# HGRN2 near scores as 32x32 diagonal blocks, levels 6 and 7 as single blocks, and one 256-column ones product in stick-breaking attention

## The reference

```
b = cumsum(log f)
scores[t,s] = sum_d q[t,d] * k[s,d] * exp(b[t,d] - b[s,d])      (s <= t)
o = scores @ v   (the reference does it chunk by chunk with a carried state)
```

```
within = cumsum(log_keep, axis=keys, reverse=True) - log_keep
later  = cumsum(block totals, reverse=True) - block totals
w = exp(log_sigmoid(z) + within + later)
```

## Time and profile before

| | |
|---|---|
| median of 3 runs | 1402.86 us (1402.77 to 1404.02) |
| the profiled execution's own time | 1402.92 us |
| its span in the profile | 1401.4 us |
| PE busy (MATMUL) | 1394.3 us, 99% of the span, 9682 records |
| PEld busy (LDWEIGHTS) | 1285.5 us, 92% |
| DVE busy | 1030.6 us, 74% |
| ACT busy | 754.0 us, 54% |
| POOL busy | 143.4 us, 10% |

### The profile page before, as it was taken

The page is one execution under the profiler, slowest core; times in us unless marked ns, Lnnn a source line. Parts: engine busy times, 40 slices in busy tenths (PEclk is TensorE's granted clock), DMA queues, the critical chain, the costliest instruction groups (busy, mean ns, idle before and its releaser), DMA issues.

```text
span 1401.4 us, 27481 instructions
## 1 busy us (share of the span) xinstructions
PE 1394.3 (99%) x9682; PEld 1285.5 (92%) x9682; DVE 1030.6 (74%) x1409; ACT 754.0 (54%) x1050; POOL 143.4 (10%) x190
## 2 busy tenths in 40 slices
PE   9999999999999999999999999999999999999999
PEld 8999999999999999988888888888888888888888
DVE  7898866699898777776687777777777776445453
ACT  7584777654543454545555555555555554344332
POOL 1200000000000014322111111111111110000000
PEclk9999999999999999999999999999999999999999
DMA  8654545454555556665556656656656656666663
GB/s 280 191 181 168 162 153 184 147 168 165 189 178 174 195 171 223 223 192 194 170 197 196 189 186 192 192 180 193 191 187 193 190 177 194 208 185 202 194 206 109
DMA packets 75935, 261.66 MB, mean 187 GB/s; under 512 B 8736, under 2 KB 9280, under 8 KB 75872
## 3 DMA queue, kind: packets, MB, share of 16 engines
q1 hardware_dynamic: 74304, 256.41, 57.0%
q0 software_dynamic: 1424, 4.37, 1.1%
q10 hardware_dynamic: 144, 0.01, 0.0%
HBM read 258.66 MB, written 2.10 MB: 186 GB/s over the span
## 4 chain that ended last, share of the span: by engine, by line
PE 91%; DVE 6%; ACT 2%; DMA 1%; issue 0%; SPq 0%; ACTq 0%; DVEq 0%
PE bank L354 40%; PE bank L368 22%; PE bank L356 21%; PE bank L394 5%; DVE w_lo L1024 2%; PE pair L413 1%; PE bank L379 1%; DVE a_in L1257 0%; ACT gates L721 0%; ACT w_hi L711 0%; DMA x_first<-xT 0%; DVE tmp L1055 0%; DVE tmp L1048 0%; DVE x_first L1217 0%; ACT tmp L721 0%
## 5 line engine op out<-in xcount | busy, mean ns | idle before, releaser
L1024 DVE TENSOR_TENSOR w_lo<-raw,w_hi 128x1024 fp32r<-128x1024 f32 x496 | 584.6, 1189 | 305.3 <-ACT w_hi L711 301.5
L711 ACT ACTIVATE w_hi<-raw 128x1024 fp32r<-128x1024 f32 x496 | 508.3, 1030 | 417.0 <-PE bank L356 198.9
L354 PE MATMUL bank<-h,w_hi 128*128 128x512 f32 x1408 | 488.4, 390 | 0.0
L356 PE MATMUL bank<-h,w_lo 128*128 128x256 f32 x1408 | 397.1, 282 | 0.0
L368 PE MATMUL bank<-a_in,w_hi 128*128 128x256 f32 x2048 | 363.1, 281 | 0.5 <-DVE w_lo L1024 0.5
L368 PEld LDWEIGHTS bank<-a_in,w_hi 128*128 128x128 f32 x2048 | 311.8, 188 | 5.3 <-issue 4.6
L354 PEld LDWEIGHTS bank<-h,w_hi 128*128 128x128 f32 x1408 | 264.2, 188 | 55.4
L368 PE MATMUL bank<-a_in,w_lo 128*128 128x256 f32 x1024 | 285.5, 279 | 0.0
L356 PEld LDWEIGHTS bank<-h,w_lo 128*128 128x128 f32 x1408 | 266.1, 189 | 0.0
L354 PE MATMUL bank<-act,w_hi 128*128 128x512 f32 x660 | 228.8, 390 | 0.0
L368 PEld LDWEIGHTS bank<-a_in,w_lo 128*128 128x128 f32 x1024 | 192.5, 188 | 0.0
(11 more groups left out here) (222 smaller groups left out, 1370.3 us busy)
## 6 DMA issues: line engine op xcount, KB each, us to landing
raw<-w_up SPq DMA_DIRECT2D x176, 512.0 KB, 3.8
raw<-w_in SPq DMA_DIRECT2D x156, 512.0 KB, 4.3
raw<-w_down SPq DMA_DIRECT2D x80, 512.0 KB, 4.2
raw<-w_out SPq DMA_DIRECT2D x32, 512.0 KB, 4.2
raw<-w_br SPq DMA_DIRECT2D x16, 512.0 KB, 3.5
raw<-w_br SPq DMA_DIRECT2D x16, 256.0 KB, 3.4
raw<-w_down SPq DMA_DIRECT2D x16, 256.0 KB, 2.7
x_first<-xT SPq DMA_DIRECT2D x8, 256.0 KB, 6.6
```

Source lines behind the costliest of these rows:

```text
L354: pe.matmul(bank[b][:, :], w[:, k * P:(k + 1) * P], a.rearrange("p a t -> p (a t)"), start=first and n == 0, stop=False, skip_group_check= ...
L356: mm = pe.matmul(bank[b][:, 0:SEQ], l[:, k * P:(k + 1) * P], a[:, 0, :], start=False, stop=last and n == len(blocks) - 1, skip_group_check ...
L711: act_e.activation(w_hi[s][:, 0:blocks * P], raw[s][:, 0:blocks * P], ACT.Copy).then_inc(hi_ready, 1)
L1024: ve.tensor_tensor(w_lo[s][:, w], raw[s][:, w], w_hi[s][:, w].bitcast(F32), ALU.subtract).then_inc(lo_ready, 1)
```

## The change

The near part (levels 0 to 5) is cut into 32x32 diagonal blocks in place of 64x64: 4 heads x 8 blocks = 32 products per level, with 32 stationary and 32 moving columns, in four groups of 32 columns of the array. Level 6 becomes its own 32x32 blocks (first quarter's keys with second quarter's queries: 16 products in two column groups), and level 7's eight 64x64 products are spread over two column groups. `NEAR`, `level_mask` and the diagonal mask become 32 wide. VectorE writes levels 6 and 7 straight into `T2[6]`, with two copies each; ScalarE copies `NEAR` in four pieces of 32 rows, one tile earlier; GpSimd zeroes two more corners. In stick-breaking, the two `ones` products of 128 columns become one of 256 columns, whose output has two runs of 128 in PSUM, and they come after the `lower` products.

```diff
+QUARTER = P // 4
-        level_mask = sb("level_mask", [P, LEVELS, HALF], U8)
-        eye_half = sb("eye_half", [P, HALF])
+        level_mask = sb("level_mask", [P, LEVELS - 2, QUARTER], U8)
+        eye_quarter = sb("eye_quarter", [P, QUARTER])
...
+                def blocks(keys, queries):
+                    return [((i * QUARTER, (i + 1) * QUARTER, (4 * b + h) * QUARTER, (4 * b + h + 1) * QUARTER),
+                             keys[:, h, (4 * b + i) * QUARTER:(4 * b + i + 1) * QUARTER],
+                             queries[:, h, (4 * b + i) * QUARTER:(4 * b + i + 1) * QUARTER], True, True)
+                            for b in range(2) for h in range(HEADS) for i in range(4)]
...
-                    ops = [((j * HALF, (j + 1) * HALF, (4 * b + h) * HALF, (4 * b + h + 1) * HALF),
-                            T4[2][:, h, (2 * b + j) * HALF:(2 * b + j + 1) * HALF],
-                            group(HG_Q)[:, h, (2 * b + j) * HALF:(2 * b + j + 1) * HALF], True, True)
-                           for b in range(2) for h in range(HEADS) for j in range(2)]
+                    ops = blocks(T4[2], group(HG_Q))
...
+                    if k < LEVELS - 2:
+                        ops = blocks(W, W)
+                    elif k < LEVELS - 1:
+                        ops = [((2 * j * QUARTER, (2 * j + 1) * QUARTER, (4 * b + h) * QUARTER, (4 * b + h + 1) * QUARTER),
+                                W[:, h, (4 * b + 2 * j) * QUARTER:(4 * b + 2 * j + 1) * QUARTER],
+                                W[:, h, (4 * b + 2 * j + 1) * QUARTER:(4 * b + 2 * j + 2) * QUARTER], True, True)
                                for b in range(2) for h in range(HEADS) for j in range(2)]
                     elif k < LEVELS:
-                        ops = [((0, HALF, (4 * b + h) * HALF, (4 * b + h + 1) * HALF), W[:, h, 2 * b * HALF:(2 * b + 1) * HALF],
-                                W[:, h, (2 * b + 1) * HALF:(2 * b + 2) * HALF], True, True) for b in range(2) for h in range(HEADS)]
+                        ops = [((b * HALF, (b + 1) * HALF, h * HALF, (h + 1) * HALF), W[:, h, 2 * b * HALF:(2 * b + 1) * HALF],
+                                W[:, h, (2 * b + 1) * HALF:(2 * b + 2) * HALF], True, True) for h in range(HEADS) for b in range(2)]
...
-                    pe.wait_ge(S("hg_within"), 2)
-                    pe.wait_ge(S("hg_zero"), 1)
+                    pe.wait_ge(S("hg_within"), 4)
+                    pe.wait_ge(S("hg_zero"), 3)
...
-                        ops += [((0, P, i * SEQ + P, (i + 1) * SEQ), ones[:, :], x[:, 512 + i * P:512 + (i + 1) * P], False, e == 1)
-                                for e, x in enumerate(parts) for i in range(2)]
                         ops += [((0, P, 512, 768), lower[:, :], x[:, 512:768], e == 0, e == 1) for e, x in enumerate(parts)]
-                        fp32_product(f"within{hh}", ops)
+                        out_ = start_product(f"within{hh}")
+                        for (p0, p1, c0, c1), lhsT, rhs, start, stop in ops:
+                            pe.matmul(out_[p0:p1, c0:c1], lhsT, rhs, start=start, stop=stop, skip_group_check=True)
+                        second = out_[:, 0:512].rearrange("p (i t) -> p i t", i=2)[:, :, P:SEQ]
+                        for e, x in enumerate(parts):
+                            mm = pe.matmul(second, ones[:, :], x[:, 512:768].rearrange("p (i t) -> p i t", i=2), start=False, stop=e == 1,
+                                           skip_group_check=True)
+                        mm.then_inc(product_done, 1)
...
-                if n == AT["lev6"] + 2:
-                    wait_taken(act_e, "lev6")
-                    act_e.wait_ge(S("hg_levels"), LEVELS - 1)
-                    for j in range(2):
-                        rows = slice(j * HALF, (j + 1) * HALF)
-                        act_e.activation(T2[6][rows, :, j * HALF:(j + 1) * HALF], NEAR[rows, :, :], ACT.Copy).then_inc(S("hg_within"), 1)
+                if n == AT["lev5"] + 3:
+                    wait_taken(act_e, "lev5")
+                    act_e.wait_ge(S("hg_levels"), LEVELS - 2)
+                    for i in range(4):
+                        rows = slice(i * QUARTER, (i + 1) * QUARTER)
+                        act_e.activation(T2[6][rows, :, rows], NEAR[rows, :, :], ACT.Copy).then_inc(S("hg_within"), 1)
...
                 if step == 1:
-                    ts("masks", row, row, float(HALF), float(HALF), ALU.is_ge, ALU.mult)
-                    tt("masks", row, place, row, ALU.subtract)
+                    for size in (HALF, QUARTER):
+                        ts("masks", part, row, float(size), float(size), ALU.is_ge, ALU.mult)
+                        tt("masks", row, row, part, ALU.subtract)
...
-                        ps = product(f"lev{k}")[:, 0:512].rearrange("p (s t) -> p s t", t=HALF)
-                        if k and k < LEVELS:
+                        ps = product(f"lev{k}")[:, 0:256].rearrange("p (s t) -> p s t", t=QUARTER)
+                        if k and k < LEVELS - 2:
                             ve.wait_ge(S("hg_levels"), k)
...
                         elif k < LEVELS - 1:
-                            ins = ve.copy_predicated(NEAR, bc(level_mask[:, k:k + 1, :], full), ps)
+                            issue(ve.tensor_copy(T2[6][0:QUARTER, :, QUARTER:HALF], ps[0:QUARTER, :, :]), "hg_far")
+                            ins = ve.tensor_copy(T2[6][HALF:HALF + QUARTER, :, HALF + QUARTER:P], ps[HALF:HALF + QUARTER, :, :])
                         elif k < LEVELS:
-                            ins = ve.tensor_copy(T2[6][0:HALF, :, HALF:P], ps[0:HALF, :, :])
+                            ps = product("lev7")[:, 0:256].rearrange("p (h t) -> p h t", t=HALF)
+                            issue(ve.tensor_copy(T2[6][0:HALF, 0:HEADS, HALF:P], ps[0:HALF, :, :]), "hg_far")
+                            ins = ve.tensor_copy(T2[6][0:HALF, HEADS:2 * HEADS, HALF:P], ps[HALF:P, :, :])
...
-            link(pool, pool.memset(T2[6][HALF:P, :, 0:HALF], 0.0), "hg_zero")
+            for rows, cols in ((slice(HALF, P), slice(0, HALF)), (slice(QUARTER, HALF), slice(0, QUARTER)),
+                               (slice(HALF + QUARTER, P), slice(HALF, HALF + QUARTER))):
+                link(pool, pool.memset(T2[6][rows, :, cols], 0.0), "hg_zero")
```

More of the change, by code:

```diff
@@ L672, in layer @@
         HG_FF, HG_QQ, HG_II, HG_GG, UU, SQ, SK = (group(g) for g in (HG_F, HG_Q, HG_I, HG_G, S5_U, SB_Q, SB_K))
-        NEAR = T[0][:, 512:1024].rearrange("p (s t) -> p s t", t=HALF)
+        NEAR = T[0][:, 512:768].rearrange("p (s t) -> p s t", t=QUARTER)
         Z = tmp[:, 0:2, :].rearrange("p a b -> p (a b)")[:, 0:1536]
@@ L1155, in masks @@
                 ve.wait_ge(S("iota"), 4)
-                diff, xor = T[4][:, 0:P].bitcast(I32), T[4][:, P:P + HALF].bitcast(I32)
-                place, row = T[4][:, 2 * P:2 * P + HALF].bitcast(I32), T[4][:, 3 * P:3 * P + HALF].bitcast(I32)
-                upper_half = T[4][:, 4 * P:4 * P + HALF]
+                diff, xor = T[4][:, 0:P].bitcast(I32), T[4][:, P:P + QUARTER].bitcast(I32)
+                row, part = T[4][:, 2 * P:2 * P + QUARTER].bitcast(I32), T[4][:, 3 * P:3 * P + QUARTER].bitcast(I32)
+                above = T[4][:, 4 * P:4 * P + QUARTER]
                 if step == 0:
@@ L1162, in masks @@
                 if step == 1:
-                    ts("masks", row, row, float(HALF), float(HALF), ALU.is_ge, ALU.mult)
-                    tt("masks", row, place, row, ALU.subtract)
-                    tt("masks", upper_half, xor, row, ALU.is_gt)
-                    tt("masks", eye_half[:, :], xor, row, ALU.is_equal)
+                    for size in (HALF, QUARTER):
+                        ts("masks", part, row, float(size), float(size), ALU.is_ge, ALU.mult)
+                        tt("masks", row, row, part, ALU.subtract)
+                    tt("masks", above, xor, row, ALU.is_gt)
+                    tt("masks", eye_quarter[:, :], xor, row, ALU.is_equal)
                     link(ve, ve.tensor_tensor(xor, xor, row, ALU.bitwise_xor), "masks")
@@ L1169, in masks @@
                     ts("masks", lower[:, :], diff, 0.0, None, ALU.is_lt)
-                for k in range(1, 4) if step == 1 else range(4, LEVELS - 1):
-                    stt("masks", level_mask[:, k, :], xor, float(2 ** (k - 1)), upper_half, ALU.is_ge, ALU.mult)
+                for k in range(1, 4) if step == 1 else range(4, LEVELS - 2):
+                    stt("masks", level_mask[:, k, :], xor, float(2 ** (k - 1)), above, ALU.is_ge, ALU.mult)
             def mixers(n):
@@ L1234, in mixers @@
                             tt("hg_segments", pre[1], pre[1], bc(pre[0][:, :, h - 1:h], shape), ALU.add)
-                full = [P, 8, HALF]
+                full = [P, 8, QUARTER]
                 for k in range(LEVELS + 1):
@@ L1238, in mixers @@
                         wait_product(ve, f"lev{k}")
-                        ps = product(f"lev{k}")[:, 0:512].rearrange("p (s t) -> p s t", t=HALF)
```

(18 more changed lines are left out.)

4 lines of the change are left out of this document (removed).

## The result

The changed kernel takes 1418.65 us (median of 5 runs, 1418.28 to 1418.84) against 1402.86 (1402.63 to 1404.02): ratio 1.0111, 95% interval 1.0099 to 1.0122. It is 15.8 us slower; forecast were 1400.7 and a range of 1399.2 to 1405.0. The profiled execution took 1418.28 us, its span 1416.7.

A forecast was written before the change was run, and what follows sets the result against it. TensorE, busy 1394.3 of 1401.4 us, was taken as the bound, with VectorE up to level 2. Terms: -0.64 - 1.11 - 0 - 0.42 = -2.17, taking 1402.92 to 1400.7 us; range 1399.2 to 1405.0.

The forecast's parts named there:

- the masks' smaller size: VectorE's masks before level 2: 12 operations of 32 columns in place of 11 of 64, 0.12 us less.
- D: Rival: something else, an unseen conflict of 32-column groups or slow narrow copies, beyond 1406 us; chance 0.05.
- A level's product: TensorE's near product of 64 records: 15 x 37 ns + 160 ns = 0.71 us, saving 0.37 per product.
- Rival A: Issue is the bound, record starts 29 ns apart, so a level's product takes 1.99 us; total 1405.8, chance 0.17.
- the lower end: Most favourable end for a level's product on TensorE: 0.52 us saved, against 0.91 lost at the other end.
- rival B: Level products stay as long as they are, through issue near 15 ns or fixed cost per record; 1401.9 us, chance 0.18.
- Level 7: TensorE's level 7 product goes from 16 steps of 64 columns to 8, 0.49 us shorter.
- the shorter products of levels 5, 6 and 7: Their 1.23 us saved on TensorE becomes wait at levels 6 to 8, behind VectorE's chain; nothing gained.
- a sign by which I had called the forecast wrong: In the changed profile, TensorE's summed waits for VectorE's L1228, which writes level factors, staying at 1.6 us.
- up to level 2: VectorE is the bound there: smaller evictions at levels 0 and 1 save 0.52, masks 0.12, together 0.64 us.
- Levels 2 to 4: Queues are tied to TensorE again, so each level's 0.37 us counts in full: 1.11 us saved.
- The ones products: Stick-breaking's within products on TensorE: 256-column ones in place of 128-column pairs save 0.21 us each, twice, 0.42.

The follow-up runs named there:

- e1: Changed kernel with an unused tensor of 448 bytes per partition behind the diagonal mask, putting later tensors back at their old addresses; 1400.76 us (ratio 0.9986).
- g4: Changed kernel without the new ones products (level part alone), with 448 unused bytes for the old placement; 1401.16 us (ratio 0.9988 against the kernel before).
- g3: Kernel before with only the ones products of 256 columns added, no tensor moved; 1402.90 us (ratio 0.9999).

## Why the prediction was wrong

**The step that failed** is none of the sum's terms but what the sum took for granted: that instructions which the diff does not touch keep their duration. The sum took the stream's 0.35 us for three products, 0.117 us each, as given, and so put the stream at a change of nothing, without a reason; the masks' smaller size entered only as 0.12 us less of VectorE's time. The runs showed 0.36 us in place of 0.35 (0.1200 against 0.1167 each in the branch stage) and 18 us in all, once the moving operands stood 448 bytes lower. The input projection alone has 1,024 such periods (2048 w_hi products, two to a period), so each 10 ns on one is 10 us. None of my rivals held it; D, beyond 1406, had 0.05 and named other causes. The range was too narrow for a diff that changes allocations in front of all the operands.

**A level's product: right.** 0.71 us were forecast; level 0 takes 0.69, level 2 0.69. Rival A, starts 29 ns apart (1.99 us), is refuted: 64 records in 0.69 us leave 11 ns each, the tail included. The fast starts in product ss were the right row, not the longest run seen. That run spoke against A already: at level 2 of the kernel before the records start in pairs, 6 to 7 ns apart and soon 59 ns from pair to pair, so 29 ns was an average of the two. At level 2 of the changed kernel the first four records start 6 to 7 ns apart, and later ones 6 to 12. The 37 ns for a record of 32 columns in the sum, the 0.52 of the lower end and rival B's fixed cost per record were estimates of mine: no run shows by itself what a step owes to its columns and what is fixed. What the traces show is the whole step: under way, the records of one column group start 32 ns apart with 32 columns (level 2 after), 58 with 64 (level 7 before) and 112 with 128 (level 8 before and after), and the first step is longer, 52, 106 and 213. By an estimate from 32 and 58, 32 columns more cost 26 ns, and 6 are left. At level 2 the last record starts 0.57 us after the first and the stream goes on 0.13 later, where the forecast had 15 x 37 = 0.56 and 0.16; the product is 0.39 shorter than before. Level 7 took 0.62 in two column groups, 0.46 less, forecast 0.49. Level 6, at 0.63, saves 0.45 where 0.37 were taken.

**What reaches the end: the path right, the agreement of the sum in part luck.** In e1, the changed kernel at the old placement, TensorE's timeline:

```profile
107.92 0.76 PE L415 MATMUL pair<-tmp 128*32 128x32 f32 x64 [1.42 <-DVE tmp L1242]
...
145.07 0.76 PE L415 MATMUL pair<-tmp 128*32 128x32 f32 x64
...
157.37 0.70 PE L415 MATMUL pair<-tmp 128*32 128x32 f32 x32
...
170.38 0.69 PE L415 MATMUL pair<-tmp 128*64 128x64 f32 x16 [0.92 <-DVE tmp L1242]
...
183.17 1.16 PE L415 MATMUL pair<-tmp 128*128 128x128 f32 x8 [0.70 <-DVE tmp L1242]
```

and its waits:

```profile
PE pair L415 <- DVE tmp L1242: 3.0, 3, 1.4
```

From level 5's product to level 8's it is 183.17 - 145.07 = 38.10 us. Before, level 5 started at 147.54 and level 8 at 185.56, 38.02 us:

```profile
147.54 1.15 PE L413 MATMUL pair<-tmp 128*64 128x64 f32 x32
```

So the shorter products of levels 5, 6 and 7 bought nothing: the waits at 7 and 8 grew from 0.45 to 1.62, as forecast (some 1.5, part of it at level 6, where the profile shows a shift but no wait). VectorE's chain sets level 8, and g4's 1.8 us is in line with it. In the changed kernel itself these waits sum to 1.5 us (0.56, 0.51, 0.41), a sign by which I had called the forecast wrong; there the slower stream gave VectorE the time, and e1, at the old pace, has the 3.0.

Level 2 starts at 107.92 in place of 109.11, 1.19 earlier, not 0.64. Of this 0.41 is there before the masks, at VectorE's `lo` in front of them (43.29 against 43.70), and goes back to the first loads: VectorE's seventh operation starts at 8.60 in e1 and 9.36 before. It starts at 8.3 to 9.5 us in the traces of this case, most often earlier in variants of the changed kernel (median 8.9) than of the kernel before (9.2), which no run explains. At the norm's root it is 0.63 (59.32 against 59.95), so the masks gave 0.22 in place of 0.12. (Five level masks are written in place of six, and 12 operations at 0.22 are 2.64, not 2.60.) The other 0.56 up to level 2 were forecast as 0.52. (VectorE's own waits from the masks to level 2 are, before, 2.27 us for the norm's root and 0.16 behind each of L1243 and L1245, which read PSUM.) Levels 2 to 4 gave 1.28 (level 5 starts at 145.07 in place of 147.54) where 1.11 were forecast. From level 5 to 8 came nothing, as forecast.

**The ones products: right in the profile, unproven in time.** The shape costs 0.47 in place of 0.68 in the changed kernel, as worked out. In g3, against before, the next product of the branches starts 0.43 us earlier than where within0 began would give (within0 at 270.01 for 270.21, the next at 283.16 for 283.79). At 327 us 0.23 of that is left (326.69 for 327.12), so the stream in between took some back, and not all of the 0.42 counts. In the median the part alone gave 0.08, with an interval from 1.4 faster to 1.1 slower.

**The sum.** e1 is 2.2 us faster and the forecast was 2.17, but that they agree so closely is luck. The levels gave 0.1 to 0.2 more than forecast in each of two stages, the ones products some 0.2 less, 0.4 was there before any edited instruction, and from 334 to 374 us e1's stream ran at 0.353 a period where the kernel before held 0.350, which cost 0.37. What the runs do show is that the miss of 18 us is placement: e1 has none of it. How the pace comes to depend on it is not settled. The runs show that the distance between moving operands and weights counts, with the same time 256 bytes further on in the one pair tried, that w_lo and w_hi each add a part, and that stages differ in which distance is good. That TensorE's two reads meet is a guess. No run looked inside a single product. Distance 64 is known from the kernel before alone, and distances between the multiples of 32 were not tried.

## What to carry to other kernels

When a diff changes the size of any tensor, ask which addresses move: here 448 bytes of shrunken masks cost 1.3% (18 us, of which the edit gave 2 back) in stages that no edit touched, and unused bytes undid it. Before judging a change of a TensorE-bound kernel, compare the period of an untouched product in both traces; if it differs, restore the placement and only then measure the change. Once an operand's distance to its weights is known to matter, sweep it in steps of 32 bytes per stage: here that was worth 2.3 to 2.8 us, no less than the change with its 1.9 to 2.2.

## What the hardware showed that I had not expected

- TensorE's pace with 128x256 and 128x512 float32 products depends on where moving operands lie against weights: the branch stage, 576 products of 256 columns, took 67.2 us at distance 32 and 69.1 at 96 (0.1167 against 0.1200 us each), and the up projection, with products of 512 and 256 columns, 488.6 at 32 and 493.2 at 96. The input projection went from 389.5 to 401.7, 3%, with no other change than unused bytes. Moving operands that start at multiples of 512 bytes were among the dear ones (1417.0 at distance 128).
- At one placement the same products ran at one of two steady paces (0.340 or 0.353 us for three at distance 192, 0.350 or 0.353 at 32) and changed between them only where the stream was interrupted.
- 64 float32 records of 32x32 blocks in four column groups pass in 0.69 us, the first four starting 6 to 7 ns apart.
